# A hybrid decoder step on one core: the routing stage's one-hot matrices divided among GpSimd, ScalarE and VectorE

## The reference

```python
def block(xb):                                   # peer_ffn
    q = (xb @ w_q).reshape(PEER_BLOCK, P_HEADS, 2, P_HALF)
    s = jnp.einsum('thpd,hpkd->thpk', q, sub_keys)
    s1, i1 = lax.top_k(s[:, :, 0], P_TOPK)       # 16 of 128 first keys
    s2, i2 = lax.top_k(s[:, :, 1], P_TOPK)       # 16 of 128 second keys
    cand = s1[..., :, None] + s2[..., None, :]
    top, pos = lax.top_k(cand, P_TOPK)           # 16 pairs (i, j) for each of 8 heads
    g = softmax(top)
    act = gelu(einsum('td,thkd->thk', xb, u[idx]))
    return einsum('thk,thkd->td', g * act, v[idx])
```

## Time and profile before

| | |
|---|---|
| median of 3 runs | 2794.08 us (2788.88 to 2794.98) |
| span of the profiled execution, first to last instruction | 2791.7 us |
| median less span | 2.4 us |
| routing stage, layer 0 | 743.47 to 882.76 us of the span |
| routing stage, layer 1 | 2256.9 to 2396.8 us of the span |
| mean granted TensorE clock, whole span | 0.958 of full speed |

### The profile page before, as it was taken

The page is one execution under the profiler, slowest core; times in us unless marked ns, Lnnn a source line. Parts: engine busy times, 40 slices in busy tenths (PEclk is TensorE's granted clock), DMA queues, the critical chain, the costliest instruction groups (busy, mean ns, idle before and its releaser), DMA issues. The chain is left out here.

```text
span 2791.7 us, 50744 instructions
## 1 busy us (share of the span) xinstructions
PE 2530.5 (91%) x17672; PEld 2236.5 (80%) x17672; DVE 1823.1 (65%) x3955; ACT 1552.8 (56%) x3124; POOL 263.3 (9%) x240
## 2 busy tenths in 40 slices
PE   6978999999867999997989998899999976899997
PEld 3658988888756999997765534798899975899997
DVE  6844789866798555557244455349885479755555
ACT  5635655676696555556413542255556579555554
POOL 0000444100000000000001110014440000000000
PEclk8989999999988999999989999999999988999999
DMA  6743444577301455553206986344445510355452
GB/s 235 256 135 139 155 162 152 209 251 260 136 0 47 180 181 180 180 181 126 64 30 247 344 327 243 121 162 155 159 164 175 180 59 0 108 179 181 180 180 106
DMA packets 65102, 455.79 MB, mean 163 GB/s; under 512 B 8656, under 2 KB 8864, under 8 KB 10224
## 3 DMA queue, kind: packets, MB, share of 16 engines
q1 hardware_dynamic: 52128, 379.61, 38.5%
q0 software_dynamic: 11120, 73.29, 6.8%
q10 hardware_dynamic: 1760, 1.68, 0.2%
HBM read 415.27 MB, written 39.27 MB: 163 GB/s over the span
## 5 line engine op out<-in xcount | busy, mean ns | idle before, releaser
L824 ACT ACTIVATE w_parts<-ring 128x512 fp32r<-128x512 f32 x1376 | 851.4, 630 | 856.0 <-PE ps L423 767.0
L1199 DVE TENSOR_TENSOR w_parts<-ring,w_parts 128x512 fp32r<-128x512 f32 x1232 | 853.8, 704 | 606.1 <-ACT w_parts L824 597.3
L423 PE MATMUL ps<-h_hi,w_parts 128*128 128x264 f32 x5376 | 1022.7, 289 | 83.3 <-DVE w_parts L1199 58.0
L423 PEld LDWEIGHTS ps<-h_hi,w_parts 128*128 128x128 f32 x5376 | 854.9, 191 | 123.7 <-issue 68.7
L423 PE MATMUL ps<-h_lo,w_parts 128*128 128x264 f32 x2688 | 770.7, 287 | 0.0
L423 PE MATMUL ps<-g_parts,w_parts 128*128 128x264 f32 x6144 | 749.6, 284 | 7.5 <-DVE g_parts L1495 7.5
L423 PEld LDWEIGHTS ps<-g_parts,w_parts 128*128 128x128 f32 x6144 | 749.3, 189 | 7.8 <-issue 7.8
L423 PEld LDWEIGHTS ps<-h_lo,w_parts 128*128 128x128 f32 x2688 | 515.4, 192 | 2.0
L423 PE MATMUL ps<-SCR 128*128 128x128 f32 x1056 | 185.5, 331 | 92.4 <-DVE SCR L1466 85.2
L1126 POOL TENSOR_TENSOR w_parts<-ring,w_parts 128x512 fp32r<-128x512 f32 x144 | 210.9, 1466 | 479.6 <-ACT w_parts L824 479.2
L423 PEld LDWEIGHTS ps<-SCR 128*128 128x128 f32 x1056 | 158.9, 231 | 118.8 <-issue 87.9
(11 more groups left out here) (176 smaller groups left out, 1473.3 us busy)
## 6 DMA issues: line engine op xcount, KB each, us to landing
ring<-in_stream SPq DMA_DIRECT2D x362, 1024.0 KB, 4.8
BIG<-in_C POOLq DMA_DIRECT2D x32, 1024.0 KB, 8.5
out_C_s<-BIG POOLq DMA_DIRECT2D x32, 1024.0 KB, 5.9
out_C_p<-BIG POOLq DMA_DIRECT2D x16, 256.0 KB, 2.3
x<-in_x ACTq DMA_DIRECT2D x1, 1056.0 KB, 15.0
out_y<-BIG POOLq DMA_DIRECT2D x1, 1056.0 KB, 4.2
consts<-in_consts ACTq DMA_DIRECT2D x1, 256.0 KB, 10.4
BIG<-in_gates POOLq DMA_DIRECT2D x1, 192.0 KB, 2.7
```

Of the source, the lines that this page charges most:

```text
L423: return nc.tensor.matmul(out, lhsT, rhs, start=start, stop=stop, skip_group_check=shared)
L824: return nc.scalar.activation(to, of, f, **kw_)
L1199: tt(w_lo[:, j % HALVES, :], half_of(n, half), w_hi[:, j % HALVES, :].bitcast(F32), ALU.subtract).then_inc(lo_ready[half], 1)
```

## The change

GpSimd makes `oh_i` for all four tokens of a group. ScalarE makes `oh_j` for three of the four, VectorE for the fourth, with a compare against one operand of one column. A new semaphore, `oh_j_last_ready`, tells TensorE of VectorE's part. GpSimd's loop is unrolled in Python, so its 264 instructions a layer have fixed addresses; it stands in the queue behind `low_rows` of the layer.

```diff
+        BY_ACT = 3
@@ TensorE, route @@
                     pe.wait_ge(oh_j_ready[l], r * OH + (s + 1))
+                    pe.wait_ge(oh_j_last_ready[l], r * OH + (s + 1))
@@ ScalarE, build @@
-                    for i in range(4):
+                    for i in range(BY_ACT):
                         last = func(oh_j[s][:, i, :], iota, ACT.Abs, scale=-1.0,
                                     bias=pickT[:, 1, bass.ds(r * (4 * OH) + (4 * s + i), 1)])
                     last.then_inc(oh_j_abs[l], 1)
                     act.wait_ge(oh_j_abs[l], r * OH + (s + 1))
-                    func(flat(oh_j[s]), flat(oh_j[s]), ACT.Relu, scale=-1.0, bias=1.0).then_inc(oh_j_ready[l], 1)
+                    o = flat(oh_j[s][:, 0:BY_ACT, :])
+                    func(o, o, ACT.Relu, scale=-1.0, bias=1.0).then_inc(oh_j_ready[l], 1)
@@ GpSimd, called after low_rows(0) and after low_rows(1) @@
+            def one_hots(l):
+                def build(r, s):
+                    if r > 0:
+                        pool.wait_ge(route_done[l], r * OH + (s + 1 - OH))
+                    for i in range(4):
+                        t = bass.ds(r * (4 * OH) + (4 * s + i), 1)
+                        last = nc.gpsimd.tensor_scalar(oh_i[s][:, i, :], iota, pickT[:, 0, t], pickT[:, 2, t],
+                                                       ALU.is_equal, ALU.mult)
+                    last.then_inc(oh_i_ready[l], 1)
+                pool.wait_ge(pickT_ready[l], 1)
+                for s in range(OH):
+                    build(0, s)
+                for r in range(1, GROUPS // OH):
+                    for s in range(OH):
+                        build(r, s)
+                for s in range(GROUPS % OH):
+                    build(GROUPS // OH, s)
@@ VectorE, build @@
-                    for i in range(4):
+                    for i in range(BY_ACT, 4):
                         t = bass.ds(g * 4 + i, 1)
-                        last = ts(oh_i[s][:, i, :], iota, pickT[:, 0, t], pickT[:, 2, t], ALU.is_equal, ALU.mult)
-                    last.then_inc(oh_i_ready[l], 1)
+                        last = ts(oh_j[s][:, i, :], iota, pickT[:, 1, t], None, ALU.is_equal)
+                    last.then_inc(oh_j_last_ready[l], 1)
```

More of the change, by code:

```diff
@@ L345, in decoder_step @@
         oh_j_ready = [sem(f"oh_j_ready{l}") for l in range(2)]
+        oh_j_last_ready = [sem(f"oh_j_last_ready{l}") for l in range(2)]
         route_done = [sem(f"route_done{l}") for l in range(2)]
@@ L1135, in _ @@
             low_rows(0)
+            one_hots(0)
             pool.wait_ge(x_ready, 2 * NC)
@@ L1166, in _ @@
             low_rows(1)
+            one_hots(1)
             pool.wait_ge(y_ready, 1)
```

## The result

The changed kernel takes 2927.44 us (median of 4 runs, 2926.39 to 2929.68) against 2791.98 us before: 1.0486 times as long, 95% interval 1.0473 to 1.0498. It is 135 us slower where 56 us faster was forecast, and lies outside the range (2705 to 2860).

A forecast was written before the change was run, and what follows sets the result against it. VectorE was taken to bound the routing stages; with GpSimd's 1.56 us and TensorE's 1.92 at the low clock, the period falls from 2.07 to 1.65 us, over 65 steps x 2 layers 55 to 56 us saved: 2738 us, range 2705 to 2860.

The forecast's parts named there:

- What bounds the kernel now: In the two routing stages VectorE is the bound, 97% busy with a 2.02 us period per group; ScalarE close behind.
- VectorE and ScalarE's new periods: Routing stage, per group after the change: VectorE 2.02 to 1.25 us, ScalarE 1.83 to 1.43 us.
- GpSimd's price: One 128x128 one-hot on GpSimd in the routing stage was put at 0.39 us, four at 1.56 us a group.
- On a line between these ... 0.39 us: GpSimd one-hot priced between a one-column MEMSET (0.09 us) and a 512-column TENSOR_TENSOR (1.29 us), 2.35 ns a column.
- The bounds 0.24 and 1.29 us: GpSimd one-hot: 0.24 us if one input halves the slope, 1.29 us if all is a cost per instruction.
- the point of no gain: GpSimd price per one-hot where the routing stage gets longer: 0.45 us with VectorE's block added, 0.52 without.
- GpSimd becomes the bound and the stage gets longer: Rival, routing stage: by VectorE's ratio 1.87 a GpSimd one-hot takes 0.49 us, giving 2811 us; chance 0.22.
- The mutual block: GpSimd and VectorE one-hots block each other for a whole instruction: up to 0.39 us on VectorE, nothing counted on GpSimd.
- `weigh` shuts GpSimd out: Rival, routing stage: GpSimd can't run beside VectorE's `weigh`, period 2.81 us, 96 us more, 2890; chance 0.08.
- The clock term: TensorE in the routing stage: 28% of the time at the low clock, 1.92 us a group there, period 1.65 us.
- a sum with 28% at the low one (2725: Rival, routing stage: ScalarE's 1.43 us sets the period, 1.54 us with the low clock's share, 69 us saved; chance 0.23.
- The wait ahead in GpSimd's queue: GpSimd's new wait for the routing stage costs nothing: the next instruction in its queue waited until 1264.44 anyway.

The follow-up runs named there:

- no_pool: Changed kernel, but GpSimd makes no weighted one-hots and VectorE all four, besides the fourth token's second one; 2817.31 us, 1.0094 of before.
- pool_two: Changed kernel, but GpSimd makes two of a group's four weighted one-hots and VectorE the other two; 2741.77 us, 0.9822 of before.
- tt_price: Changed kernel, but four TENSOR_TENSOR subtractions replace GpSimd's four one-hots, so the one-hot isn't computed; 2712.90 us, 0.9718 of before.
- pool_one: Changed kernel, but GpSimd makes one of a group's four weighted one-hots and VectorE the other three; 2783.45 us, 0.9972 of before.
- forms_a: Changed kernel, but GpSimd's four one-hots take four forms: unchanged, constants as operands, no weight, two 64-column halves; 2965.09 us, one run.
- forms_b: Changed kernel, but GpSimd's four are subtract-and-multiply, TENSOR_TENSOR subtract, copy and one-operand multiply, none computing the one-hot; 2788.46 us, one run.
- pool_three: Changed kernel, but GpSimd makes three of a group's four weighted one-hots and VectorE the fourth; 2831.26 us, 1.0145 of before.

## Why the prediction was wrong, step by step

**What bounds the kernel now** was right. VectorE was the bound: one more one-hot on it (no_pool) costs 25 us over before, one fewer (pool_two) saves 49, of which the one-hot itself makes 34 (0.26 x 130).

**VectorE and ScalarE's new periods** were right. ScalarE's 1.43 us is 1.45 in tt_price. VectorE's one-hot takes 285 ns in no_pool, where GpSimd is idle (its group by line and shape follows); the 1.25 us could not be seen alone, since VectorE then always waited for another engine.

```profile
L1494 DVE TENSOR_SCALAR SCR<-consts,SCR 128x128 f32<-128x128 f32 x132 | 37.6, 285 | 0.0
```

**GpSimd's price is the step that failed.** "On a line between these ... 0.39 us" used a MEMSET for the fixed part and a TENSOR_TENSOR for the slope. The instruction was of neither form. It takes 0.774 us, of which 0.35 is fixed, where the line had 0.09, and 0.42 goes with the columns, where it had 0.30. The prediction's own sum with that value and no block, 4 x 0.774 = 3.10 us, gives 2794 + (3.10 - 2.07) x 130 = 2928, and 2927.44 was measured. The bounds 0.24 and 1.29 us held it. The range did not: it was cut at 0.58 us, although the text worked out that 0.45 to 0.52 was already the point of no gain, and the trace had no row of this form that would have preferred the lower part of the interval.

**The rival that happened** is "GpSimd becomes the bound and the stage gets longer", given 0.22. It set the price by the ratio of the two engines for a subtraction, 1.87; for this form the ratio is 0.774 / 0.26 = 3.0. The Trainium skill ("GPSIMD Engine Reference", Engine selection) gives elementwise work to VectorE and not to GpSimd; that was borne out for all four one-hots (1.0486), but not for two of the four, where the engines share the work (pool_two, 0.9822). Its exception, one input at about line rate, was not borne out: the 3.3 ns a column alone make 0.42 us for 128 columns, 1.6 times VectorE's whole 0.26.

**The mutual block** was counted at nothing on GpSimd, which held for the change: 0.774 us beside one VectorE one-hot a group, 0.775 beside none. It held by luck: the reason given was a fixed part of 0.09 us that needs no port; the fixed part is 0.35, and no run shows what needs a port. Beside several one-hots GpSimd is slowed: 1.00 us in place of 0.79 in pool_one, 0.855 on average beside three a group in pool_two; whether by a port isn't shown. VectorE loses less: its one-hot takes 300 ns on average beside a GpSimd that never stops, 285 beside none. The "whole instruction" read from the earlier trace rows doesn't carry over to this pair; for two TENSOR_TENSORs it stands.

**`weigh` shuts GpSimd out** is refuted: `weigh` takes 1085 ns beside a busy GpSimd (1.07 to 1.11 us before), GpSimd's instruction keeps its 0.79 us beside it in pool_one, and in the changed kernel the 528 take 785 ns on average and 780 at the least although `weigh` runs for a third of the period.

**The clock term** was wrong in both directions. It took 28% of the stage at the low level as given; the changed kernel had the low level throughout, tt_price and pool_two the high one. For the change it costs nothing visible, as 2.07 us of matmuls fit into 3.09. For the two faster kernels the high clock is worth some 12 us in tt_price beyond a sum with 28% at the low one (2725 against 2712.9), and in pool_two some 5 (0.04 us x 130) of the 16.

**The wait ahead in GpSimd's queue** cost nothing, as worked out.

## What to carry to other kernels

Price a moved operation by a row of the same form on the same engine; a row of another form can be off by a factor of two, as here. Where none exists, compare the price at which the move stops paying (here 0.45 to 0.52 us) with the whole interval of the unknown, before shifting all of the work: a share of it is safer, since the slow engine then runs beside the old one. Here half of the one-hots on GpSimd saves 49 us and all of them cost 135.

## What was unexpected in the hardware

- On GpSimd a 128x128 fp32 TENSOR_SCALAR with two operations takes 785 ns (the changed kernel), with one operation 600 to 612 (forms_a, forms_b), a TENSOR_TENSOR 394 and a copy 287 (forms_b), though the TENSOR_TENSOR has a second input of 128 columns (one column, repeated) and the TENSOR_SCALAR has none.
- A `weigh`, which reads PSUM and SBUF, leaves GpSimd's TENSOR_SCALAR at 0.79 us; beside VectorE's one-hots it takes 1.00 (pool_one, median 0.96).
- The granted TensorE clock differed from kernel to kernel with the same matmuls in the stage: from 770 to 800 us it was 1.00 in tt_price and pool_two, 0.83 in pool_one, 0.73 in no_pool, 0.67 in pool_three and 0.50 in the changed kernel, in the order of their periods. In the changed kernel the low clock costs nothing visible, in the two fast ones the high clock is part of the gain.
